# One decoder step on one core: staging of the cache keys, the layer norm's place, and the order of the prompt's score maps

## The chip, the core and the metric

The kernel runs on one core of a Trainium2 chip. The metric is the device time of one execution in microseconds (us), median of three runs. Engines are named as the profile names them: PE (TensorE) with its weight load PEld, DVE (VectorE), ACT (ScalarE), POOL (GpSimd) and SP (SyncE), which issues most transfers. Each engine works through its own program in order; semaphores order them against each other.

## The reference

One inference step of a one-layer hybrid decoder, in float32, for a prompt of 1024 tokens and for 8 samples of 8 new tokens with 1024 cached positions each:

```
xn = RMSNorm(x);  z = xn @ w_in      # 2560 columns: q 512, k 512, v 512, u 512, va 512
B: for each of 4 heads, two maps m = 1, 2 of 64 dimensions:
     p_m = softmax(q_m k_m^T / 8 + rel)          # causal; rel is a bias by distance
     o   = (p_1 - lambda * p_2) v;  RMSNorm(o) per head * (1 - lambda_init)
A: u, va = GELU(..);  u * (tril(W_s[g]) LayerNorm(va) + b[g])   # chunks of 128 positions, 4 groups
x = x + RMSNorm(concat(B, A) @ w_out)
x = x + RMSNorm((silu(g) * u') @ w_down), (g, u') = conv3(RMSNorm(x) @ w_up)
```

The samples attend to `cache_k[page_table]` and `cache_v[page_table]`: 64 pages of 128 tokens x 512 columns (256 KB a page), and to their own keys. k, v, the convolution's state and the samples' normalised va rows are outputs too.

## The kernel before

Products are made of three matmuls each: an operand is split into a rounded part and the rest (`_hi`, `_lo`), and hi x hi, hi x lo and lo x hi are added in PSUM. Tokens: 1088 columns, the samples' 64 first; nine tiles (`STEPS`), eight of 128 prompt rows and one of the samples' 64.

**Projections.** The 2560 columns of w_in are ten groups of 256: va 0, va 1, u 0, u 1, k 0, k 1, q 0, q 1, v 0, v 1 (`GROUPS`). A va or v group is nine jobs (one for each token tile, 24 matmuls of 256 columns), the other groups six jobs (24 matmuls of about 364 columns). Between the k jobs stand the nine gate jobs (the spatial product of A, one for each tile), between the q jobs the nine krow jobs (k turned for its output). Each job has a PSUM bank, the eight in turn; ACT takes the banks of va, u and krow (L941, L947, L952), DVE those of k, q, v and gate. At the first job of a group, ACT and DVE split the weights of the next one (L741, L747), whose raw halves SP loads two places ahead.

Beside this the samples' cached keys are brought into the layout that their scores need. 32 pairs of pages go through: SP loads a pair (`load_pair`, L784 on, into `k_tok[0]` or `k_tok[2]`, from pair 25 on into `k_tok[0]` alone), DVE transposes it in blocks of 32 into `k_tok[1]` (`turn_pair`, L1534 on), ACT stores it to `keys_t` in HBM (`store_pair`). `PAIR_SETS` and `PAIR_AT` say at which job: five pairs in each of the groups va 1 to k 1, four in q 0, three in q 1. In all three programs the pair stands at its job's place: DVE's transpose waits for all stores before it, ACT's store for the transpose, and ACT has it before the take of the next job.

The layer norm of va stands on DVE at the first job of u 0: for each tile `layer_stats` (DVE), a root (POOL), `center` (DVE), gain and bias (POOL, L1372 and L1374), one tile after the other. The gate jobs need its result.

**Attention.** 32 steps (`NSTEP`): four heads of eight query tiles; a step's width is 1 to 8 key tiles (ascending, in the last head descending). Steps over four tiles are wide and have a far part (banks 0 and 2) and a near part (1 and 3) for each map. For a step: PE makes the scores of both maps (`scores`); DVE takes the far part's minimum (`far_max`, L1553), adds the bias to the near part and takes its minimum (`near_max`, L1562); ACT takes exponents with row sums (`exponent`, L1027); DVE mixes the maps (`mix`, L1572 to L1577); PE turns the mix (`turn`), ACT copies it (`take_turned`, L1037), PE multiplies it with v (`weigh`, L2210); ACT squares the output (`out_square`, L1043), POOL makes the factor (L1391 to L1395), DVE scales it (`out_norm`, L1584). The scores of a step wait until both exponents of the last user of their bank are done. PE's order in step i: scores(i), the samples' scores of half a unit (`smp_scores`, L2247), weigh(i-2), turn(i-1). weigh(i-2) waits for out_norm(i-3). ACT: out_square(i-3), take_turned(i-2), exponent(i, 0), exponent(i, 1). DVE: where the scores have a free bank early, near_max(i, 0) or both far_max; mix(i-1); then the minima that are left, with out_norm(i-3) among them.

The samples' keys come back from `keys_t` in 16 units of 1 MB (`load_keys`, L810 on): unit 0 into `kt_first`, the others in turn into `kt_a`, `kt_mid`, `kt_b`, which lie in the place of the low parts of the activations and so are free only when all jobs are done. Unit u is used in steps 2u and 2u+1 (unit 0 in step 1). The cached values come in eight loads of 2 MB (`load_values`), two places.

Behind it stand w_out (L2338), the FFN (L2395, L2460) and the last norms, which the change leaves as they are.

## Time and profile before

| | us |
|---|---|
| median of 3 runs (1407.11 to 1408.3) | 1407.67 |
| the profiled execution | 1407.97 |
| its span | 1406.2 |
| PE busy in the span | 1331.6 (95%) |
| DVE, ACT, POOL busy | 722.5, 445.1, 168.7 |
| mean granted clock of TensorE | 0.981 |

Projections: the last v job begins at 318.98 us; attention: to 489.27 us, where the first product with w_out stands in the chain; w_out: to 603.29 us; then the FFN. The span is what the profile shows of one execution, from its first to its last instruction; the device time is 1.77 us longer. Busy is a union of times; PE and PEld overlap. In the tables of windows the counts in brackets are instructions, the clock is the mean that was granted to TensorE (1.00 is full), and the DMA share is that of the 16 DMA engines, which can read a little over 1. In groups by line the idle time is that of the engine just before these instructions, with what ended it. A wait is put down to the last of the things waited for.

### The profile page before, as it was taken

The page shows a single profiled execution, that of the slowest core. Times are in us where ns is not written, and L with a number is a line of the kernel's source. Part 1 is how long each engine was busy: PE and PEld are TensorE (multiplying, and loading weights), DVE is VectorE, ACT ScalarE, POOL GpSimd, SP SyncE. Part 2 cuts the span into 40 slices and gives each one's busy share as a digit, 9 for nine tenths or more (in the row PEclk, how much of TensorE's full clock was granted, in tenths as well). Part 3 has the DMA queues.
Part 4 walks back from the last instruction along what each step waited for, and adds up shares of the span by engine and source line. Part 5 has one row for each costly group of instructions (what it writes and reads, how often), then busy time and mean ns, then how long its engine had stood idle before and what let it go on. Part 6 is the DMA issues. An engine that isn't in the chain of part 4 may idle for free.

```text
span 1406.2 us, 21878 instructions
## 1 busy us (share of the span) xinstructions
PE 1331.6 (95%) x8386; PEld 1199.4 (85%) x8386; DVE 722.5 (51%) x1175; ACT 445.1 (32%) x751; POOL 168.7 (12%) x323
## 2 busy tenths in 40 slices
PE   7995798997887999999999999999999999999998
PEld 6995798994564788899898989898989999999986
DVE  6432453315668756455645454545453635454456
ACT  6301101203555754335131323232323223232332
POOL 2253000002222221120000000000000000000003
PEclk9998799998999999999999999999999999999999
DMA  7525676638879453242111110202020201110116
GB/s 261 167 75 172 226 226 206 197 88 222 212 178 269 126 171 120 83 120 75 31 60 30 40 50 21 69 15 75 15 75 15 74 15 60 30 60 27 48 46 131
DMA packets 115672, 146.97 MB, mean 105 GB/s; under 512 B 8012, under 2 KB 83445, under 8 KB 115605
## 3 DMA queue, kind: packets, MB, share of 16 engines
q1 hardware_dynamic: 107865, 122.30, 29.5%
q10 hardware_dynamic: 6748, 20.24, 4.0%
q0 software_dynamic: 992, 3.54, 1.5%
q8 instruction: 42, 0.69, 0.2%
q14 instruction: 25, 0.20, 0.0%
HBM read 114.06 MB, written 31.47 MB: 103 GB/s over the span
## 4 chain that ended last, share of the span: by engine, by line
PE 77%; DMA 7%; DVE 6%; POOL 4%; issue 3%; ACT 1%; SPq 1%; ACTq 0%; DVEq 0%; POOLq 0%
PE PS L2395 37%; PE PS L2460 16%; PE PS L2117 8%; PE PS L2338 7%; DMA keys_t<-k_tok 6%; DVE k_tok L1542 2%; PE PS L2210 2%; PE PS L2475 2%; PE PS L2490 2%; POOL small L1393 1%; DMA x_in<-in_x_prompt_dram 1%; PE PS L2270 1%; PE PS L2172 1%; POOL va L1372 1%; DVE w_lo L747 1%
## 5 line engine op out<-in xcount | busy, mean ns | idle before, releaser
L2395 PE MATMUL PS<-act_lo,wu_hi 128*128 128x364 f32 (+1 forms) x1056 | 346.4, 328 | 0.0
L2395 PE MATMUL PS<-act_hi,wu_lo 128*128 128x364 f32 (+1 forms) x1056 | 346.0, 328 | 0.0
L2395 PE MATMUL PS<-act_hi,wu_hi 128*128 128x364 f32 (+1 forms) x1056 | 345.9, 328 | 0.0
L2395 PEld LDWEIGHTS PS<-act_hi,wu_hi 128*128 128x128 f32 x1056 | 198.5, 188 | 0.5
L2395 PEld LDWEIGHTS PS<-act_lo,wu_hi 128*128 128x128 f32 x1056 | 198.1, 188 | 0.4
L2395 PEld LDWEIGHTS PS<-act_hi,wu_lo 128*128 128x128 f32 x1056 | 198.3, 188 | 0.0
L1877 DVE TENSOR_TENSOR y_acc<-y_acc,PS 128x512 f32<-128x512 f32 x162 | 111.2, 686 | 116.0 <-PE PS L2460 116.0
L2460 PE MATMUL PS<-wd_hi,g_hi 128*128 128x512 f32 x324 | 130.1, 402 | 0.0
L2460 PE MATMUL PS<-wd_lo,g_hi 128*128 128x512 f32 x324 | 128.0, 395 | 0.0
L2117 PE MATMUL PS<-act_hi,w_hi 128*128 128x364 f32 (+1 forms) x288 | 99.6, 346 | 20.7 <-DVE w_lo L747 10.0
L2460 PE MATMUL PS<-wd_hi,g_lo 128*128 128x512 f32 x288 | 114.0, 396 | 0.0
L1263 ACT CAST g_hi<-conv 128x1088 fp32r<-128x1088 f32 x21 | 23.1, 1102 | 245.8 <-PE PS L2460 189.7
L2117 PE MATMUL PS<-act_lo,w_hi 128*128 128x364 f32 (+1 forms) x288 | 97.5, 339 | 0.0
L2117 PE MATMUL PS<-act_hi,w_lo 128*128 128x364 f32 (+1 forms) x288 | 97.4, 338 | 0.0
L1435 POOL COPY stT<-hsw 128x32 f32 (+1 forms) x22 | 12.6, 571 | 696.8 <-DVE conv L1913 654.7
L1902 DVE SCALAR_TENSOR_TENSOR conv<-h_gate,cwi,conv 128x1023 f32<-128x1023 f32 x22 | 28.3, 1285 | 131.8 <-ACT conv L1251 131.8
L1542 DVE STREAM_TRANSPOSE k_tok<-k_tok 128x1024 f32<-128x1024 f32 x32 | 39.8, 1244 | 101.4 <-DMA keys_t<-k_tok 68.8
L2117 PE MATMUL PS<-w_hi,act_hi 128*128 128x256 f32 x288 | 82.0, 285 | 2.2 <-DVE act_lo L1492 1.3
L2117 PE MATMUL PS<-w_hi,act_lo 128*128 128x256 f32 x288 | 80.9, 281 | 0.0
L2117 PE MATMUL PS<-w_lo,act_hi 128*128 128x256 f32 x288 | 80.4, 279 | 0.0
L2460 PEld LDWEIGHTS PS<-wd_hi,g_hi 128*128 128x128 f32 x324 | 60.8, 188 | 21.5 <-DVE y_acc L1877 8.3
L1027 ACT ACTIVATE prob<-PS,small 128x128 f32<-128x128 f32 (+7 forms) x64 | 47.3, 740 | 91.9 <-DVE small L1562 46.0
(287 smaller groups left out, 2319.9 us busy)
## 6 DMA issues: line engine op xcount, KB each, us to landing
wu_raw<-in_w_up_dram SPq DMA_DIRECT2D x44, 512.0 KB, 3.8
k_tok<-in_cache_k_dram SPq DMA_DIRECT2D x64, 256.0 KB, 3.2
keys_t<-k_tok ACTq DMA_DIRECT2D x32, 512.0 KB, 2.9
vpage<-in_cache_v_dram SPq DMA_DIRECT2D x64, 256.0 KB, 3.9
wd_raw<-in_w_down_dram SPq DMA_DIRECT2D x22, 512.0 KB, 5.3
w_raw<-in_w_in_dram SPq DMA_DIRECT2D x20, 512.0 KB, 6.3
kt_a<-keys_t SPq DMA_DIRECT2D x20, 256.0 KB, 5.4
kt_mid<-keys_t SPq DMA_DIRECT2D x20, 256.0 KB, 7.2
```

What stands on the lines that cost most here:

```text
L1027: nc.scalar.activation(dst, score_cols(i, m), ACT.Exp, scale=-1.0, bias=nmax[:, i % 4, m:m + 1], accum_out=prob_sum[:, i % 4, m:m + 1]).th ...
L1263: nc.scalar.copy(g2_hi[e][:, NS:] if last else g_hi[:, e, NS:], conv[:, 1, :]).then_inc(g_hi_ready, 1)
L1542: nc.vector.transpose(turned, blocks).then_inc(ktok_turned, 1)
L1877: nc.vector.tensor_tensor(dst, dst, PS[:, 6 + half, :], ALU.add).then_inc(ybank_free, 1)
L1902: nc.vector.scalar_tensor_tensor(conv[:, half, NS + 1:], h[:, NS:NTOK - 1], w1, conv[:, half, NS + 1:], ALU.mult, ALU.add).then_inc(tap1_r ...
L2117: mm = nc.tensor.matmul(out, lhs, rhs, start=(i == 0), stop=(i == len(pairs) - 1))
L2210: mm = nc.tensor.matmul(PS[:, out_bank(i), 0:DV], at_sb[:, i % 2, P * k:P * k + P], v_all[:, k, DV * h:DV * h + DV], start=(k == 0), stop= ...
L2338: mm = nc.tensor.matmul(PS[:, Y_BANK[t % 2] + half, :], a[:, k, wide(TILES[t])], w[:, 512 * half:512 * half + 512], start=(first and j == ...
L2395: mm = nc.tensor.matmul(PS[:, 3 * half + c, 0:kept(c)], a[:, half, k, :], b[:, k, KEPT[c]], start=(j == 0), stop=(j == len(parts) - 1))
L2460: mm = nc.tensor.matmul(PS[:, 6 + half, :], g, w[:, e, 512 * half:512 * half + 512], start=(j == 0), stop=(j == len(parts) - 1))
L2475: nc.tensor.matmul(PS[:, LAST_BANK[t % 4] + half, :], g, w[:, e, 512 * half:512 * half + 512], start=(j == 0), stop=False)
L2490: mm = nc.tensor.matmul(PS[:, LAST_BANK[t % 4] + half, :], g, w[:, 512 * half:512 * half + 512], start=False, stop=(e == 1 and j == len(pa ...
```

## The change

- Three places for loaded pairs instead of two: `k_tok[0..2]` where q will lie (pairs 0 to 24), `k_tok[3..5]` where va lay (pairs 25 to 31). The load of pair 25 waits for all gates and for the store of the samples' va. Pair n is loaded when pair n-3 is transposed.
- Two places for transposed pairs (`k_turned`); the transpose waits for the store two before. ACT issues a store one job later.
- Tile s of the layer norm stands at the job 1 + s behind the first of u 0, its centering one job later.
- Unit 1 of the keys has its own place (`kt_second`, in the place of `vpage1`) and is loaded when group v 1 begins; the others follow in turn in `kt_mid`, `kt_b`, `kt_a`. The load of values 1 waits for the samples' scores of step 3.
- `scores` goes map by map; each map waits only for its own map's exponent of the bank's last user.
- DVE takes the first map's minimum (and out_norm(i-3)) before the mix of the last step.
- ACT squares output i-2 between the two exponents of step i.
- PE makes the samples' scores before the prompt's in each step from 2 on that isn't a multiple of 4.

```diff
-    k_tok = [at("k_tok0", 2 * ACT_BYTES + 1024, [P, 2, 512]), at("k_tok1", SCRATCH, [P, 2, 512]),
-             at("k_tok2", keep.at, [P, 2, 512])]
+    k_turned = [at("k_turned0", 2 * ACT_BYTES + 1024, [P, 2 * 512]), at("k_turned1", SCRATCH, [P, 2 * 512])]
...
+    k_tok = [at(f"k_tok{i}", a + 4096 * (i % 3), [P, 2, 512]) for i, a in enumerate(3 * [R0] + 3 * [R2 - STEPS * AW * 4])]
...
-    kt = [kt_first] + [kt_a, kt_mid, kt_b] * 5
+    kt = [kt_first, at("kt_second", V1, [P, 2, 4, 2, H, 32])] + [kt_mid, kt_b, kt_a] * 5
...
-    TOK_OF = [2 * (n % 2) if n < 25 else 0 for n in range(NPAIR)]
+    NQ_PAIR = 25
+    TOK_OF = [n % 3 if n < NQ_PAIR else 3 + n % 3 for n in range(NPAIR)]
...
+    NORM_AT = [first_of[2] + 1 + s for s in range(STEPS + 1)]
...
         def load_pair(n):
             b = TOK_OF[n]
-            if tok_uses(n):
-                sp.wait_ge(ktok_turned, max(m for m in range(n) if TOK_OF[m] == b) + 1)
-            else:
+            if n == 0:
                 sp.wait_ge(nrm_ready, STEPS)
+            if n == NQ_PAIR:
+                sp.wait_ge(gate_mul, STEPS)
+                sp.wait_ge(sgu_stored, 16)
+            if n >= 3:
+                sp.wait_ge(ktok_turned, n - 2)
...
         def load_keys(u):
-            if u == 1:
-                sp.wait_ge(kt_loaded[0], 64)
-            if u >= 4:
+            if u in (2, 3):
+                sp.wait_ge(kt_loaded[u - 2], 64)
+            if u >= 5:
                 sp.wait_ge(sscore_ready, 2 * (u - 3) + 2)
...
             elif b == 0:
                 sp.wait_ge(gated_kept, AG)
+            else:
+                sp.wait_ge(sscore_ready, 4)
...
         load_keys(0)
+        sp.wait_ge(job_ready, first_of[len(GROUPS) - 1])
+        load_keys(1)
...
         sp.wait_ge(job_ready, len(jobs))
-        load_keys(1)
...
-            if n in PAIR_AT:
-                store_pair(PAIR_AT.index(n))
+            if n - 1 in PAIR_AT:
+                store_pair(PAIR_AT.index(n - 1))
...
         for i in range(NSTEP):
-            if i >= 3:
-                out_square(i - 3)
...
             if i >= 1:
                 exponent(i, 0)
+                if 2 <= i < NSTEP - 1:
+                    out_square(i - 2)
...
         def turn_pair(n):
             b = TOK_OF[n]
-            dve.wait_ge(slot_loaded[b], 48 + 32 * (tok_uses(n) + 1))
-            if n >= 1:
-                dve.wait_ge(ktok_stored, 16 * n)
+            dve.wait_ge(slot_loaded[b % 3], slot_count(n))
+            if n >= 2:
+                dve.wait_ge(ktok_stored[n % 2], 16 * (n // 2))
...
-                if g == 2:
-                    for s in range(STEPS):
-                        layer_stats(s)
-                        if s >= 1:
-                            center(s - 1)
-                    center(STEPS - 1)
...
             if n in PAIR_AT:
                 turn_pair(PAIR_AT.index(n))
+            if n in NORM_AT:
+                s = NORM_AT.index(n)
+                if s < STEPS:
+                    layer_stats(s)
+                if s >= 1:
+                    center(s - 1)
...
         for i in range(NSTEP):
-            if i >= 2 and early(i):
+            if i >= 2:
                 if wide_step(i):
                     far_max(i, 0)
-                    far_max(i, 1)
+                    if early(i):
+                        far_max(i, 1)
+                    if i >= 3:
+                        out_norm(i - 3)
+                    near_max(i, 0)
                 else:
-                    near_max(i, 0)
-            if i == 3:
-                out_norm(i - 3)
+                    if i - 1 not in JOINED:
+                        near_max(i, 0)
+                    if i >= 3:
+                        out_norm(i - 3)
             if i >= 1:
                 mix(i - 1)
...
+            if i >= 2:
                 if wide_step(i) and not early(i):
-                    far_max(i, m)
...
+                    far_max(i, 1)
+                if i - 1 in JOINED:
+                    near_max(i, 0)
+                near_max(i, 1)
...
-            for j, (c, e) in enumerate(parts):
...
-                user = bank_user(i, 1 if second_bank(i) else j)
-                if user >= 0:
-                    pe.wait_ge(prob_ready, 2 * user + 2)
-                for m in range(2):
-                    d = slice(DH * m, DH * m + DH)
+            for m in range(2):
+                d = slice(DH * m, DH * m + DH)
+                for j, (c, e) in enumerate(parts):
...
+                    user = bank_user(i, 1 if second_bank(i) else j)
+                    if user >= 0:
+                        pe.wait_ge(prob_ready, 2 * user + m + 1)
...
+        def samples_first(i):
+            return i >= 2 and i % 4 != 0
+
         for i in range(NSTEP):
+            if samples_first(i):
+                smp_scores(i)
             if i in PARTED:
                 scores(i, 1)
...
-            if i >= 1:
+            if i >= 1 and not samples_first(i):
                 smp_scores(i)
```

## Rows read from the trace of the kernel before

**Rows 1.** Windows from:to, length, busy PE PEld DVE ACT POOL, clock, DMA share, GB/s

```profile
46.40:110.70 64.30, 64.30 (x457) 64.04 (x456) 21.70 (x34) 9.21 (x19) 24.40 (x32) 1.00 0.38 124
110.70:230.00 119.30, 89.27 (x507) 87.76 (x507) 53.37 (x63) 14.03 (x21) 8.04 (x9) 0.86 0.67 218
...
320.00:340.00 20.00, 13.29 (x144) 7.00 (x143) 10.63 (x39) 8.06 (x33) 5.84 (x9) 0.74 0.88 189
340.00:489.20 149.20, 126.45 (x1311) 84.51 (x1311) 104.61 (x294) 88.73 (x240) 38.71 (x82) 0.99 0.77 202
...
130.00:140.00 10.00, 2.04 (x13) 1.74 (x11) 1.64 (x3) 2.29 (x4) 0.00 (x0) 0.78 0.81 277
...
340.00:360.00 20.00, 15.57 (x118) 9.63 (x118) 15.26 (x39) 11.78 (x29) 5.33 (x11) 1.00 1.08 299
...
490.00:500.00 10.00, 9.93 (x51) 7.92 (x51) 8.44 (x24) 7.50 (x21) 3.04 (x6) 1.00 0.94 320
```

**Rows 2.** Waits of PE by length: total, times, longest

```profile
PE PS L2172 <- ACT prob L1027: 10.9, 13, 1.0
PE PS L2117 <- DVE w_lo L747: 10.7, 2, 10.0
PE PS L2210 <- DVE o_nrm L1584: 9.3, 16, 1.0
PE PS L2117 <- ACT uT L947: 7.4, 1, 7.4
PE PS L2095 <- DVE kT L1718: 6.2, 1, 6.2
...
PE PS L2247 <- DMA kt_a<-keys_t: 4.5, 1, 4.5
...
PE PS L2247 <- ACT s_prob L1065: 2.5, 3, 1.0
```

**Rows 3.** Groups by line in the projections: count, busy, mean ns, idle before, releasers

```profile
L1542 DVE STREAM_TRANSPOSE k_tok<-k_tok 128x1024 f32<-128x1024 f32 x32 | 39.8, 1244 | 101.4 <-DMA keys_t<-k_tok 68.8 <-DMA k_tok<-in_cache_k_dram 32.5
...
L947 ACT ACTIVATE uT<-PS 128x364 f32<-128x364 f32 (+1 forms) x12 | 5.7, 473 | 79.7 <-DVE k_tok L1542 79.3 <-PE PS L2117 0.4
```

**Rows 4.** Chain that ended last: start, length, engine or transfer

```profile
54.41 2.93 DMA keys_t<-k_tok
...
67.33 7.17 DMA keys_t<-k_tok
...
82.35 1.29 POOL va L1372
...
111.91 1.27 POOL va L1372
...
221.43 5.38 PE PS L2117 x24
227.24 3.94 PE PS L2117 x24
...
339.54 0.56 POOL small L1393
```

**Rows 5.** DMA issues: size and median time to landing

```profile
keys_t<-k_tok ACTq DMA_DIRECT2D x32, 512.0 KB, 2.9
```

**Rows 6.** Busy time of each engine in three steps of the second head

```profile
386.26:391.41 5.15, 3.80 (x29) 2.31 (x29) 3.77 (x10) 2.80 (x8) 1.45 (x3) 1.00 1.09 296
391.41:397.08 5.67, 4.35 (x32) 2.65 (x32) 4.18 (x11) 3.19 (x9) 1.58 (x3) 1.00 1.00 280
397.08:403.20 6.12, 5.44 (x39) 3.40 (x39) 5.61 (x13) 4.04 (x10) 1.72 (x3) 1.00 0.67 152
```

**Rows 7.** Groups by line, in the attention

```profile
L1027 ACT ACTIVATE prob<-PS,small 128x128 f32<-128x128 f32 (+7 forms) x64 | 47.3, 740 | 91.9 <-DVE small L1562 46.0 <-PE PS L2117 43.6 <-DVE prob L1577 2.2
...
L1393 POOL TENSOR_TENSOR small<-small 128x1 f32<-128x1 f32 x32 | 27.8, 869 | 2.7
L1577 DVE SCALAR_TENSOR_TENSOR prob<-prob,small,prob 128x128 f32<-128x128 f32 (+7 forms) x32 | 27.0, 843 | 1.1
```

More of the change, by code:

```diff
@@ L517, in _program @@
     ktok_turned = sem("ktok_turned")
-    ktok_stored = sem("ktok_stored")
+    ktok_stored = [sem(f"ktok_stored{i}") for i in range(2)]
     kt_loaded = [sem(f"kt_loaded{i}") for i in range(3)]
@@ L631, in _program, with slot_count, kt_count @@
     PAIR_AT = [jobs_of(k + 1)[j * len(jobs_of(k + 1)) // len(pairs)] for k, pairs in enumerate(PAIR_SETS) for j in range(len(pairs))]
-    def tok_uses(n):
-        return TOK_OF[:n].count(TOK_OF[n])
+    NORM_AT = [first_of[2] + 1 + s for s in range(STEPS + 1)]
+    def slot_count(n):
+        return 48 + 32 * (sum(b % 3 == TOK_OF[n] % 3 for b in TOK_OF[:n]) + 1)
     def kt_place(u):
-        return max(u - 1, 0) % 3
+        return (u - 2) % 3 if u >= 2 else u
+    def kt_count(u):
+        return 64 * (sum(kt_place(v) == kt_place(u) for v in range(u)) + 1)
     ring, ring_taken = [], []
@@ L834, in _ @@
         sp.wait_ge(w_lo_ready, 2 * len(GROUPS))
-        sp.wait_ge(ktok_stored, 16 * NPAIR)
+        for i in range(2):
+            sp.wait_ge(ktok_stored[i], 16 * NPAIR // 2)
         load_keys(0)
+        sp.wait_ge(job_ready, first_of[len(GROUPS) - 1])
+        load_keys(1)
         v_jobs = [n for n, job in enumerate(jobs) if job[0] == "v"]
```

22 lines of the change are left out of this document (8 added, 14 removed).

## The prediction

> **What bounds the kernel now.** I read the page first: PE is busy 95% of the span, so what can be won is PE's idle time and the time in which it runs below full clock. The table of windows says where that is: between 110.7 and 230.0 us PE is busy 89.27 of 119.30 us at a mean granted clock of 0.86, between 320 and 340 us 13.29 of 20 at 0.74, and from 340 to 489.2 us, the rest of the attention, 126.45 of 149.20 at 0.99; from 46.4 to 110.7 it has no idle time at all [rows 1]. The change does not touch what comes behind the attention. Then the waits by length name what ends each idle stretch [rows 2].
>
> In the projections these waits (w_lo 10.7, uT 7.4, kT 6.2 us) are not the work of those operations. VectorE's 32 transposes L1542 take 39.8 us and have 101.4 us of idle before them, 68.8 of it until the last store `keys_t<-k_tok` has landed, and ScalarE's 12 evictions L947 wait 79.3 us for such a transpose [rows 3]. All transposes write one tile, so each waits for the store before it; ScalarE, which issues the store, waits for the transpose before it may take PE's next bank. The chain in order of time shows the store's 2.93 to 7.17 us, and between them nine tiles of layer norm: 82.35 to 111.91 is seven of them, 4.22 us each [rows 4]. No pair of pages moves in that time. PE runs 8 banks ahead, then stands.
>
> In the attention the waits are 10.9 us for `prob` (a step's scores wait until the exponents of both maps of the step before have freed the banks), 9.3 us for `o_nrm` (a head's output waits for ScalarE's square, POOL's root and VectorE's scale), 4.5 us once for `kt_a`, 2.5 us for `s_prob` [rows 2].
>
> **The change, part by part.**
>
> *Projections: staging and layer norm.* Removed are the wait of a transpose for the store just before it (now for the one two before) and of a load for one of two places (now three). A store is issued one job later, so ScalarE takes PE's bank first. No instruction is added. PE then waits only if the mean pace of pairs is below its own. Its u job is 24 matmuls at 3.94 us [rows 4]. The ring that is left: the next job must end (4.0) and be taken (about 0.5), store n-2 lands after 2.9 by median [rows 5], transpose n takes 1.24 [rows 3]: 8.6 us for two pairs, against two jobs at 4.0 and a sixth job in each group without a pair. It fits; a store of 7.17 is 4 us late once, and the 8 banks cover it. The layer norm keeps POOL's lockstep of 4.22 us a tile, from about 83 to 125 us, now beside the pairs; its last tile is due for a gate in k1, after 150. Were that cover gone, a gate would wait a tile, 4 us. On SP's queue pair 25 is held until all gates are done and `sgu` is stored; behind it stand the weight halves of the last groups, due some 25 us later: nothing.
>
> So the idle time 119.30 - 89.27 = 30.0 us should go [rows 1], and the low clock with it. In the chain the first projection after the stall before 220 us takes 5.38 us, the next, of the same 24 matmuls, 3.94 [rows 4]; a mean of 0.86 lies between the levels 1.2 and 2.4 GHz, and the low one came behind idle stretches. The clock's cost is at most 89.27 x 0.14 = 12.5 us, and at least 5 restarts x 1.44 = 7.2; I take 9. For what stays (the first key rows wait for the last k eviction, perhaps a gate) I leave 1. Sum: 30 + 9 - 1 = 38 us, bounds 25 (the pairs keep the pace in part) and 41.
>
> *Keys of the second unit* get a place of their own and are loaded during v1. The wait of 4.5 us goes, and some of the low clock behind it: in 320 to 340 that costs at most 13.29 x 0.26 = 3.5 us [rows 1, 2]. I take 4.5 + 1 = 5.5; bounds 3 (the start's own chain of exponent, mix and turn is late next) and 8. Values 1 now wait on SP's queue until unit 1 is used (step 3), with the keys of unit 5 behind them; both are due at steps 9 and 10: nothing.
>
> *Scores map by map, the first map's minimum before the mix, the square a step earlier, the samples' scores first.* The idle time from 340 us on is 149.20 - 126.45 = 22.75 us [rows 1]. Three steps of the second head, cut at their mixes of 640, 768 and 896 columns: spans 5.15, 5.67, 6.12 us; PE busy 3.80, 4.35, 5.44; VectorE 3.77, 4.18, 5.61; ScalarE 2.80, 3.19, 4.04 [rows 6]. After the change a step cannot be shorter than VectorE's work and its handovers, some 0.4 us: 4.2, 4.6, 6.0, or about 0.95, 1.05 and 0.1 less than now; the fourth wide step is like the third, with a gap for `s_prob`.
>  Does a ring forbid it? Map 1: its exponents end, then mix (0.84 mean, 0.4 with its two small ones), half of VectorE's other work (1.4), an exponent (0.74 + 0.2) [rows 6, 7]: with handovers 4.1 us in the middle step: below 4.6. The new one: ScalarE's square stands between the exponents of the two maps and waits for the weighing, which stands behind map 1's scores on PE. That is at most 2.7 of PE's 4.35 to 5.44, a square and an exponent (0.5 and 1.0): 4.2, while PE has a turn, the samples' scores and map 0's scores of the next step to do. It fits too.
>  The `o_nrm` wait (9.3) goes whole, since POOL's 0.87 mean [rows 7] and its two short ones now have a step's time. Of the `prob` wait (10.9) the samples' and map 0's scores fill about half; of `s_prob` (2.5) I count nothing. 9.3 + 5 = 14 us of the 22.75. Bounds: 3 (the waits only change places) and 20.
>  POOL's root L1393 takes 0.56 us at 339.54 but 0.87 in the mean, in steps where VectorE mixes [rows 4, 7]. The Trainium skill (SBUF — State Buffer, on the shared port pair) says that a GpSimd operation and a VectorE operation with two SBUF inputs exclude each other for a whole instruction; the mix is such a one, and the trace agrees. By that rule a root can still be held by a mix after the change; that would be some 0.5 us inside the slack of a step, and where one were late again it would be a part of rival B.
>
> *Sum.* 38 + 5.5 + 14 = 57.5 us. The profiled execution took 1407.97 us, 1.77 over its span; the median of the runs is 1407.67, 0.3 less. 1407.97 - 57.5 - 0.3 = 1350. What is behind only moves forward. The last values and rows of w_out, whose transfers fill 490 to 500 us (320 GB/s, share 0.94 [rows 1]), hang on the last steps' products, and that tail gets hardly shorter.
>
> **Rivals.**
> *A, the pairs keep part of the pace.* A pair moves 1.05 MB; with the weights that is 18.9 MB in va1, u0 and u1. PE does these in 64.3 us less one va job (2.8) and plus three u jobs (12) [rows 1]: 73.5 us, 257 GB/s. The stretch with pairs shows 218 GB/s in the mean and 277 at a share of 0.81 at best [rows 1]. At 218 they would be 13 us late, and the stalls of u1 and k0 come back: 12 us less gain, 1362. The Trainium skill (DMA: Bandwidth & Descriptors, Issuing engines are not separate DMA queues) has it that DMAs of all issuing engines interleave on the same 16 engines: more places give no rate once the share is full, as in 340 to 360 us with 299 GB/s at 1.08 [rows 1]; the trace agrees, but the stretches with pairs are below that. Chance 0.14.
> *B, the attention gains only its key wait.* Map 1's exponents then wait for the weighing, or VectorE's order sets the step: 14 becomes 1: 1363. For it: VectorE is within 0.2 us of PE in all three steps [rows 6]. Against: it idles up to 1.5 us a step. Chance 0.14.
> *C, slower.* The ring of staging: a store held a job longer, transpose and load behind it. PE has 181 us for 32 pairs, 5.65 each (projections to the end of q1). Each pair over that costs PE 32 times the excess; 58 us are eaten at 1.8 us, when the ring takes 2 x 7.45 = 14.9 us, which needs stores of 9.2 us instead of 2.9. At 10 us it is 1350 + 32 x 2.2 = 1420. The longest store in the chain has 7.17 [rows 4]. Chance 0.03. That the change does nothing, because something else holds PE at the same places: 1407, 0.01.
> *D, all idle time goes:* 41 + 8 + 20: 1339. Chance 0.13.
>
> **The numbers.** Forecast 0.55 (its own range 1342 to 1358), A 0.14, B 0.14, D 0.13, C 0.03, nothing 0.01. Range 1337 to 1368. A measurement of this kernel tells 0.2% (3 us) from no change: faster 0.96, within it 0.01, slower 0.03.
>
> **What would show it.** PE without idle and at clock 1.00 from 46 us to the end of the projections, at about 283 instead of 322 us; L1542 idle for loads or for nothing; L947 waiting for PE alone; layer norm between transposes, to about 125 us. No wait of L2247 for keys, none of L2210 for `o_nrm`, half of L2172's 10.9 us; wide steps of 4.2, 4.6, 6.0 us; PE's first L2338 near 431. Wrong in the first part if uT or w_lo still end waits of several us; in the third if PE's idle time from the fourth step on stays above 15 us.

## The result

| | before | after |
|---|---|---|
| median of the runs | 1407.99 us (1407.11 to 1408.31) | 1370.55 us (1369.76 to 1374.39) |
| profiled execution, its span | 1407.97, 1406.2 | 1369.76, 1368.0 |
| start of the samples' own scores (end of the projections) | 321.95 | 282.39 |
| from there to the first product with w_out | 167.3 | 169.0 |
| from there to the end of the span | 916.9 | 916.6 |

The ratio is 0.974 (95% interval 0.9721 to 0.976): faster, by 37 us instead of the forecast 57.5, and outside the range. The three parts of the table say where. The projections gained 39.6 us (forecast 38), the rest behind the attention moved forward unchanged, and the attention, which was to lose 19.5 us (5.5 for the keys, 14 for the new orders), became 1.7 us longer. One of the four executions of e12 below took 2351 us, in a slow state of the chip, and is not counted.

Windows of the changed kernel, with the columns of [rows 1]: the projections as there, ten of their microseconds, and the whole attention.

```profile
46.40:110.70 64.30, 64.30 (x460) 64.25 (x458) 28.40 (x35) 14.69 (x28) 16.86 (x21) 1.00 0.71 236
110.70:230.00 119.30, 119.30 (x755) 118.76 (x754) 60.67 (x80) 15.18 (x21) 20.48 (x21) 1.00 0.73 246
...
190.00:200.00 10.00, 10.00 (x64) 9.95 (x64) 2.22 (x3) 1.17 (x2) 0.00 (x0) 1.00 0.96 348
282.39:451.38 168.99, 150.31 (x1436) 98.33 (x1436) 111.90 (x326) 97.02 (x274) 32.18 (x91) 0.99 0.76 196
```

And the attention of the kernel before, in the same cut:

```profile
321.95:489.27 167.32, 137.79 (x1436) 89.71 (x1436) 113.97 (x323) 96.80 (x272) 44.62 (x90) 0.96 0.80 202
```

The second row is what [rows 1] had at 89.27 us busy and a clock of 0.86: now PE has no idle time and full clock. The last row of the first fence and the row after it are the point of this case. The same 1436 matmuls keep PE busy for 150.31 us instead of 137.79, at a clock no lower. Its idle time did fall, from 29.5 to 18.7 us, and 12.5 us of busy time came in its place. A look at idle time alone would have called this a success.

The groups that answer to [rows 3, 5, 7] (line, operation, count, busy, mean ns, idle before and its end; the last row is DMA issues):

```profile
L1557 DVE STREAM_TRANSPOSE k_turned<-k_tok 128x1024 f32<-128x1024 f32 x32 | 39.3, 1234 | 21.8 <-DMA keys_t<-k_turned 21.8
L1408 POOL TENSOR_TENSOR small<-small 128x1 f32<-128x1 f32 x32 | 18.4, 576 | 2.7
L961 ACT ACTIVATE uT<-PS 128x364 f32<-128x364 f32 (+1 forms) x12 | 5.7, 474 | 38.1 <-PE PS L2134 38.1
keys_t<-k_turned ACTq DMA_DIRECT2D x32, 512.0 KB, 4.1
```

The transposes wait 21.8 us instead of 101.4, ScalarE's takes wait for PE alone. The waits of PE by length, to be set against [rows 2]:

```profile
PE PS L2287 <- ACT s_own L1095: 4.2, 3, 1.5
PE PS L2215 <- DVE prob L1592: 4.0, 8, 1.5
PE PS L2227 <- DVE o_nrm L1599: 3.9, 7, 1.1
PE PS L2189 <- ACT prob L1042: 3.6, 3, 1.5
```

Above them stands 5.4 us for `rel_rep` at the very start, as before (5.2). `prob` fell from 10.9 to 3.6, `o_nrm` from 9.3 to 3.9, the keys' 4.5 is gone; new is `s_own`, three times about 1.4. The three steps of [rows 6], cut at the same mixes:

```profile
345.69:350.91 5.22, 4.78 (x28) 2.50 (x27) 3.82 (x10) 2.97 (x9) 0.93 (x3) 1.00 1.06 314
350.91:356.51 5.60, 5.60 (x33) 3.12 (x32) 4.22 (x10) 3.13 (x8) 0.93 (x3) 1.00 1.03 257
356.51:362.25 5.74, 4.15 (x36) 3.41 (x39) 4.53 (x13) 5.03 (x13) 0.93 (x3) 1.00 1.00 205
```

Forecast were 4.2, 4.6 and 6.0 us. In the middle one PE is busy for all of its 5.60 us, where [rows 6] have 4.35. Where the busy time comes from stands in the timeline of the scores of a 1024-column step (start, length, operation, count), first of the kernel before, then of the changed one, with the end of map 1's exponent on ScalarE:

```profile
397.10 1.99 PE L2172 MATMUL PS<-kT,qT 64*128 64x512 f32 x8 [1.00 <-ACT prob L1027]
```

```profile
353.36 3.17 PE L2189 MATMUL PS<-kT,qT 64*128 64x512 f32 x8
...
354.30 0.19 ACT L1042 ACTIVATION_READ_ACCUMULATOR prob<-PS,small 128x1 f32 x1
```

Eight equal matmul records (two for each matmul of the program) take 1.99 us in the one and 3.17 in the other. Map 0 of a head contracts over rows 0 to 63 of the array and map 1 over rows 64 to 127. Before, their records start in pairs, 7 ns apart (397.099 and 397.106), and run together. After the change map 0's start at 353.358, 353.891, 354.321 and 354.750; map 1's wait for map 1's exponent, start at 354.544 and end at 356.52, so that the two overlap in part only. The Trainium skill (TensorEngine Tiling (Array Packing), Key Properties) says that tiles of the array operate independently and can execute matmuls in parallel; the trace agrees, and the prediction had not weighed it.

More busy time is not yet a longer step, though. Map 1's exponent ends at 397.04 before and at 354.49 in the changed kernel; the last score ends 2.05 us and 2.04 us behind it. In none of the 13 wide steps whose scores are issued as a whole do the two kernels differ in this by over 0.1 us. Map 0's scores only start earlier, in time in which PE would have waited for map 1's exponent. What sets the 5.60 us is a ring (a chain of waits that closes on itself, here from one mix to the next):

```profile
350.91 1.02 DVE L1592 SCALAR_TENSOR_TENSOR prob<-prob,small,prob 128x768 f32<-128x768 f32 x1
...
351.99 0.87 PE L2215 MATMUL PS<-ident,prob 128*128 128x128 f32 x6
...
352.79 0.64 PE L2264 MATMUL PS<-kt_a,qp 128*32 128x256 f32 x8
...
355.38 0.75 DVE L1577 CUSTOM_DVE_ANT_0 PS<-PS,bias_sb,far_min 128x512 f32<-128x512 f32 x1
...
356.51 1.15 DVE L1592 SCALAR_TENSOR_TENSOR prob<-prob,small,prob 128x896 f32<-128x896 f32 x1
```

The mix of a step, its turn on PE, the samples' scores and map 0's scores of 353.36 behind it in PE's program, map 0's minimum as soon as they end (355.38), and the next mix, which now stands behind that minimum. In the kernel before, the chain that ended last has neither PE nor a mix in this stretch (start, length):

```profile
391.38 0.36 ACT PS L1043 x2
...
392.09 1.22 POOL small L1393
...
393.87 0.62 DVE PS L1562
...
394.54 0.56 DVE far_min L1553
...
396.85 0.19 ACT prob L1027
```

From the end of map 1's exponent to the end of the next one, 391.38 to 397.05, it goes over the square, POOL's factor, `out_norm`, the minima of both maps and map 1's exponent: 5.67 us, the length of the middle step in [rows 6].

### The profile page after: what moved, and what is told of

It reads as the page before. It is cut to its first block, busy times and chain, and to the rows that moved or that the text cites. A ratio compares the mean times of both kernels' runs of the same rounds, so it can differ in the third digit from the quotient of the medians.

```text
span 1368.0 us, 21879 instructions
## 1 busy us (share of the span) xinstructions
PE 1334.0 (98%) x8386; PEld 1199.9 (88%) x8386; DVE 720.4 (53%) x1175; ACT 445.5 (33%) x751; POOL 159.8 (12%) x323
## 4 chain that ended last, share of the span: by engine, by line
PE 92%; DVE 3%; issue 2%; ACT 1%; DMA 1%; SPq 0%; POOL 0%; POOLq 0%; DVEq 0%; ACTq 0%
PE PS L2418 38%; PE PS L2134 17%; PE PS L2483 16%; PE PS L2361 7%; PE PS L2189 3%; PE PS L2227 2%; PE PS L2498 2%; PE PS L2513 2%; PE PS L2264 1%; PE PS L2215 1%; PE PS L2287 1%; DVE prob L1592 1%; PE PS L2119 1%; DMA x_in<-in_x_prompt_dram 1%; PE PS L2352 1%
## 5 line engine op out<-in xcount | busy, mean ns | idle before, releaser
L2134 PE MATMUL PS<-act_hi,w_hi 128*128 128x364 f32 (+1 forms) x288 | 95.8, 333 | 0.0
L2134 PE MATMUL PS<-act_lo,w_hi 128*128 128x364 f32 (+1 forms) x288 | 94.4, 328 | 0.0
L2134 PE MATMUL PS<-act_hi,w_lo 128*128 128x364 f32 (+1 forms) x288 | 94.4, 328 | 0.0
L2483 PEld LDWEIGHTS PS<-wd_lo,g_hi 128*128 128x128 f32 x324 | 60.9, 188 | 12.3
```

The costliest lines, as they stand in the source:

```text
L2134: mm = nc.tensor.matmul(out, lhs, rhs, start=(i == 0), stop=(i == len(pairs) - 1))
L2483: mm = nc.tensor.matmul(PS[:, 6 + half, :], g, w[:, e, 512 * half:512 * half + 512], start=(j == 0), stop=(j == len(parts) - 1))
```

## The experiments

Attention is the time from the own scores to the first w_out product; idle is PE's in it; scores is the union of the 192 prompt score matmuls. Clock is the mean granted to TensorE in the attention. The last two columns are the third and the last head (steps 17 to 24 and 25 to 32, each from the end of one weighing to the end of the next, the first one counted from the own scores). All from the profiled execution, the time is the median. "Base" in the list means the changed kernel's projections and keys with the attention of before.

| kernel | time | attention | idle | scores | clock | third head | last head |
|---|---|---|---|---|---|---|---|
| before | 1408.0 | 167.3 | 29.5 | 40.6 | 0.96 | 44.5 | 40.6 |
| changed | 1370.6 | 169.0 | 18.7 | 54.4 | 0.99 | 44.5 | 47.0 |
| e1 changed, pairs with one wait | 1386.0 | 184.5 | 41.4 | 42.0 | 0.96 | 49.8 | 50.3 |
| e2 before, map by map | 1407.1 | 168.3 | 29.9 | 40.3 | 0.96 | 44.6 | 40.8 |
| e3 base | 1363.7 | 163.6 | 26.5 | 39.6 | 0.98 | 44.6 | 40.6 |
| e4 changed, pairs with own waits | 1372.9 | 173.6 | 20.2 | 54.5 | 0.97 | 45.4 | 46.2 |
| e5 base + map by map, own waits | 1362.7 | 163.8 | 16.4 | 51.3 | 0.98 | 44.6 | 40.6 |
| e6 base + early square | 1367.8 | 166.2 | 31.7 | 39.6 | 1.00 | 45.5 | 45.6 |
| e7 base + minimum ahead of mix | 1387.3 | 186.3 | 39.2 | 44.3 | 0.94 | 49.7 | 50.2 |
| e8 base + samples first | 1365.8 | 165.4 | 29.4 | 39.6 | 0.99 | 45.1 | 41.4 |
| e9 changed, mix first | 1368.4 | 167.7 | 25.3 | 48.3 | 1.00 | 45.7 | 45.4 |
| e10 base + early square in part | 1361.8 | 163.3 | 24.7 | 40.6 | 0.97 | 44.2 | 40.6 |
| e11 e10 + map by map, own waits | 1359.8 | 159.0 | 13.1 | 52.5 | 1.00 | 44.2 | 40.6 |
| e12 changed, layer norm in a block | 1383.1 | 169.0 | 18.7 | 54.4 | 0.99 | 44.5 | 47.0 |
| e13 e11 + minimum ahead of mix | 1366.3 | 166.1 | 9.1 | 58.8 | 0.97 | 42.5 | 50.5 |
| e14 e11, second unit's keys late | 1365.4 | 165.2 | 17.5 | 53.4 | 0.98 | 44.2 | 40.6 |
| e15 before + layer norm spread | 1376.9 | 166.6 | 30.5 | 40.6 | 0.97 | 44.5 | 40.6 |

The clock is a cause of its own in this list. The 15th step of the kernel before takes 1.2 us more than its 7th, which has the same products, and the clock is low in it (columns as in [rows 1]):

```profile
358.74:364.96 6.22, 4.13 (x40) 3.06 (x38) 5.23 (x22) 4.18 (x13) 1.85 (x3) 1.00 1.03 206
401.78:409.22 7.44, 5.66 (x39) 4.24 (x38) 6.39 (x27) 4.19 (x13) 1.85 (x3) 0.77 0.63 136
```

e15, with the same attention, has 6.22 us in both, e3 7.48 in both at a clock of 0.77. Which execution has it where is not explained by any edit here. Behind the first two steps the clock is full throughout in e6, e9 and e11, and in all third heads but those of e1 (23rd step 0.81) and e7 (24th, 0.81), so the third heads are the cleanest comparison: there the four edits together cost nothing (44.5 against 44.6 us), and what the changed kernel loses to e3 stands in the last head.

**e1: the changed kernel with the scores in pairs.** The loop of before inside the changed kernel: part by part, both maps together, after the exponents of both.

```
-            for m in range(2):
-                ...
-                for j, (c, e) in enumerate(parts):
-                    ...
-                        pe.wait_ge(prob_ready, 2 * user + m + 1)
+            for j, (c, e) in enumerate(parts):
+                ...
+                    pe.wait_ge(prob_ready, 2 * user + 2)
+                for m in range(2):
```

> The changed kernel with the order of the score products as before: for each part both maps one behind the other, and the wait for both exponents of the bank's last user. All else as changed. Theory 1 (the two maps read rows 0 to 63 and 64 to 127, and their matmuls ran at the same time as long as they stood next to each other; map by map they run one after the other in wide steps): the union of the score matmuls in the attention falls from 53.4 us to about 40, and the time from 1370.5 to 1357 to 1361. Theory 2 (the score order costs nothing; the square between the exponents and the minimum before the mix set the steps): 1368 to 1372.

Measured 1386.0 us, ratio 0.9854 (0.9814 to 0.9893): above both expectations. The pairs are back (scores 42.0) and the attention is 15.5 us longer. So the lost pairs can't be the cause alone: something else in the changed attention is very dear once the scores wait for both maps (e7 finds it). Its waits: `prob` 19.5 us, `prob` ahead of the turn 7.1.

**e2: the kernel before with the scores map by map**, under the wait of before.

```
-            for j, (c, e) in enumerate(parts):
+            for m in range(2):
+                ...
+                for j, (c, e) in enumerate(parts):
                     ...
                     pe.wait_ge(prob_ready, 2 * user + 2)
-                for m in range(2):
```

> The kernel before with one edit: scores map by map, still with the wait for both exponents. Theory 1: 20 wide steps of two parts lose the overlap, 0.45 to 0.9 us each on a path that has little slack: union from 39.7 to about 53 us, time 1408 to between 1416 and 1422. Theory 2: within 2 us of before, as no instruction and no wait is added.

1407.1 us, ratio 0.9995 (0.9979 to 1.001). The order of issue does nothing. The timeline row:

```profile
398.29 1.99 PE L2172 MATMUL PS<-kT,qT 64*128 64x512 f32 x8 [1.00 <-ACT prob L1027]
```

It is still 1.99 us, against the first expectation: the records start in pairs 13 ns apart (398.291, 398.305), although in the program all of map 0's matmuls stand ahead of map 1's. What takes the pair apart is thus the wait between the maps.

**e3: the changed projections and keys, all four attention edits undone.**

> The changed kernel with all attention edits but the keys' own place taken back (score order, minimum, square, samples' scores as before). Both theories: the projections' 39.6 us stay, and the keys' wait of 4.5 us and its low clock go: 1408 - 39.6 - 5.5 = 1363, so below the changed kernel. Theory 1 puts it above run e1 (the other orders gain a few us: 1363 against 1359), theory 2 puts it 7 us below e1.

1363.7 us (1360.98 to 1365.67), ratio 0.9682 (0.9646 to 0.9718): some 7 us below the changed kernel. Projections and keys do what was forecast (1407.97 - 38 - 5.5 = 1364.5), and the four attention edits together cost 7 us by the medians. In the profiled executions the attention differs by 5.4 us (169.0 against 163.6), and e3's own scores started 1.7 us earlier with the same projections.

**e4: pairs, but each map with its own wait** (the loop of e1 with `2 * user + m + 1`).

> As run e1, but each map waits only for its own exponent; the parts are still the outer loop. Theory 1: where map 1's exponent is late, map 0's far part starts alone and that pair is lost, the near pair is kept: union 40 to 47 us, time 1357 to 1364. Theory 2: as e1.

1372.9 us, ratio 0.9745 (0.9711 to 0.9778); scores 54.5. Above the first expectation. Same as the changed kernel in its pairing, as e2 leads one to expect: with a wait of its own map 1 comes later whatever the order. Its 7th, 8th and 15th steps, at a clock of 0.71 to 0.86, are together 4.7 us longer than the changed kernel's.

The next four put one attention edit each on the base of e3.

**e5: map by map with own waits.** The first loop of the diff of e1, turned round.

> The kernel with the changed projections and the attention of before (1363.7 us), with one attention edit put back: the scores go map by map, each map waiting for its own exponent. Theory A (lost pairs): the wait between the maps takes them apart, so the union of the score matmuls rises from 39.6 us to over 50 us, the idle time of TensorE falls by about as much, and the time stays within 1362 to 1369. Theory B (the square ahead of map 1's exponent is what costs): the edit alone gains what the prediction gave it, some 4 us: 1358 to 1361. Theory C (TensorE's own wait was never the bound): union and idle unchanged, 1363 to 1365.

1362.7 us (1361.34 to 1364.45), ratio 0.968 (0.9662 to 0.9699). Waits of PE in e3, then in e5:

```profile
PE PS L2187 <- ACT prob L1042: 11.3, 14, 1.0
PE PS L2225 <- DVE o_nrm L1599: 10.3, 16, 1.2
```

```profile
PE PS L2225 <- DVE o_nrm L1599: 10.9, 18, 1.2
...
PE PS L2187 <- ACT prob L1042: 0.6, 2, 0.3
```

The wait for `prob` falls by 10.7 us, the score matmuls take 11.7 us more, the time is the same. The numbers are the first expectation's; its reason, that the lost pairs eat up a gain, is not what the trace shows. The scores that moved now run during the wait, and the last score still ends 2.03 us behind map 1's exponent. Neither kernel's chain goes over this wait: between two wide steps both have the ring of the kernel before, from exponent over square, POOL's root and the minima to exponent, without PE (in e5 from 346.78 to 352.45, 5.67 us as before). An eleven-microsecond wait was filled, and it had cost nothing.

**e6: the early square.**

```
-            if i >= 3:
-                out_square(i - 3)          # head of step i
                 exponent(i, 0)
+                if 2 <= i < NSTEP - 1:
+                    out_square(i - 2)
                 exponent(i, 1)
```

> The same base (1363.7 us) with the square of step i-2 between the two exponents of step i as the only attention edit. Theory B: ScalarE waits there for the weighing, map 1's exponent and with it the next pair of scores come later, and every wide step grows: 1374 to 1386, with over 15 us of idle time ahead of the squares. Theory A: ScalarE has slack, 1362 to 1366. Theory D (the edit gains, since the square no longer stands at the head of the step): 1356 to 1361.

1367.8 us, ratio 0.9725 (0.9707 to 0.9743): 4 us slower than e3. Steps are counted here from the end of one weighing to the end of the next, 1 to 32: the 7th shrinks from 7.48 to 5.78 us, and the 9th and 17th grow from 6.33 to 7.87, the 28th from 7.66 to 8.97. The time lies above the expectation of slack in ScalarE and below that of a cost in every wide step. The last head is 5.0 us longer in all. Of the 7th's gain 1.26 us is the clock, which was 0.77 in e3. In the 9th, 17th and 28th ScalarE also copies the samples' probabilities. The changed kernel has the same; its timeline there:

```profile
368.10 2.05 PE L2227 MATMUL PS<-v_all,at_sb 128*128 128x128 f32 x16
...
370.19 0.34 ACT L1058 ACTIVATE PS<-PS,small 128x128 f32<-128x128 f32 x1 [1.86 <-PE PS L2227]
...
370.55 0.46 ACT L1042 ACTIVATE prob<-PS,small 128x256 f32<-128x256 f32 x1
...
371.46 0.21 ACT L1095 COPY s_own<-PS 64x64 f32<-64x64 f32 x1
...
371.72 1.93 PE L2287 MATMUL PS<-vpage,s_at 128*8 128x128 f32 x64 [1.46 <-ACT s_own L1095]
```

The square waits for the weighing, and behind it in ScalarE's program stand map 1's exponent and the two sample copies (`s_at`, `s_own`), for which PE then waits. In e3 `s_own` is copied at 367.58, while PE weighs.

**e7: the minimum ahead of the mix.** VectorE's loop of the changed kernel on the base of e3 (in its core):

```
             if i >= 2:
+                    near_max(i, 0)         # needs scores(i)
             if i >= 1:
                 mix(i - 1)
-                near_max(i, 0)
                 near_max(i, 1)
```

> The same base (1363.7 us) with VectorE's order of the changed kernel (first map's minimum ahead of the last step's mix) as the only attention edit. Theory A and the prediction: map 0's exponent starts earlier, but TensorE waits for both exponents, so 1361 to 1365. Theory E (the mix comes later and the turn on TensorE waits for it, the time's new bound): the wait for prob ahead of the turn rises from under 1 us to over 5 us in sum and the time to 1368 to 1376. Theory B expects 1361 to 1366.

1387.3 us (1386.79 to 1388.38), ratio 0.9859 (0.9843 to 0.9876): 23.6 us slower than e3, more than any expectation. Its chain of waits over one wide step (start, length):

```profile
351.10 0.88 DVE prob L1592
351.99 0.61 DVE far_min L1568
...
352.73 0.49 DVE PS L1577
...
354.12 0.20 ACT prob L1042
...
354.36 2.81 PE PS L2189 x8
...
357.91 0.23 DVE small L1589
...
358.16 1.02 DVE prob L1592
```

This is a ring of 7.06 us from mix to mix (5.15 in [rows 6] between the mixes of the same widths): the mix, map 1's minimum behind it in VectorE's program, map 1's exponent, the next scores which wait for it, map 0's minimum of these scores, and only then the next mix. Before, the mix ran beside the scores and was not in the ring. One microsecond of the 7.06 is the clock: it was 0.78 in this step, and the eight score records took 2.81 us instead of the 1.77 of the same step in e3. The next step, from 358.16 to 364.94 at a clock of 0.98, takes 6.78 us against 5.67. VectorE's waits show it; in e7 from 300 us on:

```profile
DVE far_min L1568 <- PE PS L2189: 26.5, 12, 3.3
```

In e3 the same wait is 1.0 us, in the changed kernel 16.2. Of the 22.8 us by which e7's attention is longer than e3's, 12.7 are idle time and 10.1 busy time of PE, with the same matmuls at a mean clock of 0.94 instead of 0.98; e6, with its scores in pairs too and full clock, needs 134.5 us where e7 needs 147.1. So the ring and a low clock share the loss. In the seven steps of the third head that e7 has at full clock (17th to 23rd) the order alone costs 2.6 us (40.5 against 37.9). The ring also explains e1, which has this order with the wait for both maps: 1386.0.

**e8: the samples' scores first.**

```
+            if samples_first(i):           # i >= 2 and i % 4 != 0
+                smp_scores(i)
             scores(i)
```

> The same base (1363.7 us) with the sample scores ahead of the step's own scores on TensorE as the only attention edit. Theory A: TensorE fills its wait for the exponents with the sample scores, which are 1.0 to 1.4 us a step where a step has them; the step's own scores and so the exponents start no later, and the time falls to 1357 to 1361. Theory F (the sample scores wait for the keys or for the sample probabilities and hold the step's scores behind them): 1366 to 1374. Theory B: 1362 to 1365.

1365.8 us, ratio 0.9703 (0.9687 to 0.9719): 2.1 us slower if anything. `prob` falls from 11.3 to 5.9 us and `o_nrm` rises from 10.3 to 16.8: the wait moved. The time lies between the third expectation and the second.

**e9: the changed kernel with the mix first** (the diff of e7 backwards).

> The changed kernel (1370.6 us) with VectorE's order of before: the last step's mix ahead of the first map's minimum; scores map by map, early square and sample scores first stay. Theory E (the minimum ahead of the mix costs whatever else is changed, since the mix then waits for the scores of the next step; it cost 23.6 us alone): 1363 to 1368. Theory G (with a wait per map it costs nothing, the early square and the samples are what is lost: singly -1.0, +4.1 and +2.1 us on 1363.7): 1368 to 1372.

1368.4 us (1367.67 to 1369.02), ratio 0.9713 (0.9695 to 0.973). What costs 23.6 us on e3 costs 2.1 us here: map 0's scores no longer wait for map 1's exponent, so their minimum is less late (VectorE waits 16.2 us for it in all instead of 26.5), and the clock is low less often. The measured value lies just inside the second expectation and 0.4 us above the first; theory E's "whatever else is changed" is wrong. In the first three heads the order costs nothing (132.2 us with it, 133.2 without); in the last, where the changed kernel's clock was low in two steps, it costs 1.6 us.

**e10: the early square in some steps only.**

```
+        def square_early(i):
+            return 2 <= i < 24 and i not in SMP_STEP     # SMP_STEP = [9, 17, 28]
```

> Projections of the changed kernel, attention of before, and the early square only in steps before 24 that take no sample output (not in 9, 17 and from 24 on). With the early square everywhere the three steps after a turned head lost 1.7 us each less, steps 9 and 17 cost 1.54 each more and the steps from 25 on 5.5 us more. Theory H (these are separate effects): 163.6 us of attention falls by 5 to 6 us and the time to 1357 to 1360. Theory I (what is won in one step is waited for in the next): 1362 to 1365.

1361.8 us (1359.14 to 1365.71), ratio 0.9667 (0.9639 to 0.9694). Between both expectations and not told apart from e3. The steps 9, 17 and from 25 on are back at e3's lengths, but the 7th and 15th keep 7.24 and 7.08 us, at clocks of 0.78 and 0.80.

**e11: the same, map by map with own waits.**

> As the run before, with the scores map by map as well. Theory J (ScalarE and VectorE set the step; TensorE's pairing only turns idle time into busy time, as where it was alone, 1362.7 against 1363.7 us): within 2 us of the run before. Theory K (with the early square, map 0's scores come earlier and pay): 3 us or more below the run before.

1359.8 us (1358.9 to 1363.73), ratio 0.9662 (0.9639 to 0.9685): the best kernel here by its median, with an attention of 159.0 us, 4.6 less than e3; it is below the changed kernel by 10.7 us, which is clear, and below e3 by 3.9, where the runs overlap. The whole attention and the second of the three steps:

```profile
281.46:440.43 158.97, 145.90 (x1436) 95.27 (x1436) 112.78 (x323) 96.02 (x272) 36.34 (x90) 1.00 0.79 207
...
345.12:350.59 5.47, 5.35 (x34) 3.21 (x32) 4.08 (x10) 3.12 (x9) 0.93 (x3) 1.00 0.95 254
```

Against e3 PE's idle time is 13.5 us less and its busy time 8.9 us more (145.9 against 137.0). The three steps are 4.95, 5.47 and 6.31 us, shorter than [rows 6] by 0.2 at most and the last one longer; the gain is in the 7th and 15th (5.78 against 7.48) and the 2nd (3.39 against 4.03). Of the 7th's and the 15th's, 1.26 us each is e3's low clock, so of the 4.6 us some 2.1 are left for the edits (an estimate: 4.6 less twice the 7.48 - 6.22 of the steps above). Between e10 and e11 the profiled attentions differ by 4.4 us, the medians by 2.0, and the runs overlap.

**e12: the changed kernel with the layer norm as one block.**

```
             if g + 1 > split:
                 dve_split_w(dve, split)
+                if g == 2:
+                    ...                    # nine tiles, one after the other
-            if n in NORM_AT:
-                ...                        # one tile
```

> The changed kernel (1370.6 us) with the layer norm as one block of nine tiles again; three staging places stay. Theory L (the layer norm's 38 us without a transpose are what stood in the way; PE is 8 banks ahead and then stands): the own scores start 15 to 30 us later, 1385 to 1400. Theory M (the single staging tile with its wait for each store was it): they start up to 8 us later, 1371 to 1379.

1383.1 us, ratio 0.9816 (0.9794 to 0.9838). The own scores start at 297.46, 15.1 us later, as the first expectation has it, though the time stays 2 us under its range. The window of [rows 1] and the chain behind the block:

```profile
110.70:230.00 119.30, 108.09 (x657) 107.00 (x656) 63.25 (x75) 19.49 (x28) 6.75 (x8) 0.94 0.81 283
```

```profile
116.30 0.88 SPq L800
...
120.87 0.91 SPq L741
121.83 10.55 DMA w_raw<-in_w_in_dram
...
134.76 7.04 PE PS L2134 x24
```

The pairs' loads stand in SP's queue until the block is over and VectorE transposes again; the next weights stand behind them, and their transfer then shares the rate with the pairs that follow: 10.55 us, while the core's transfers together ran at 375 GB/s and a share of 1.02. So the norm's block reached PE through the weights.

**e15: the kernel before with the layer norm spread**, the single staging tile kept.

> The kernel before (1407.7 us) with the layer norm's tiles spread over the jobs, the staging tile as before. The run with the new staging and the norm in one block showed the block to be worth 15 us of the 39.6. Theory S (two separate delays that add up): 1391 to 1395. Theory T (with one staging tile the pairs are late anyway, so the norm between them gains less and adds a late gate): 1396 to 1408.

1376.9 us (1376.05 to 1378.61), ratio 0.9791 (0.9769 to 0.9814), below both expectations. Own scores at 290.98: 31.0 us earlier than before.

```profile
110.70:230.00 119.30, 111.92 (x699) 111.14 (x698) 59.13 (x78) 14.94 (x21) 18.27 (x22) 0.97 0.68 219
```

The staging alone gives 24.5 us (321.95 - 297.46), the spread alone 31.0, both 39.6. They are not two separate delays: either lets the pairs catch up with what the other loses.

**e13: e11 with the minimum ahead of the mix.**

> The kernel of the part-wise early square and map-by-map scores (1359.8 us; own scores to w_out 159.0 us) with the first map's minimum ahead of the last step's mix as the only further edit. Theory E (the minimum waits for scores, and only a wait for both maps makes these late): with a wait per map it costs little, 1358 to 1363, with wide steps longer by 0.5 us and narrow ones shorter by 0.4 us, as in the changed kernel against its version with the mix first. Theory N (the order costs whatever the wait): 1370 or more.

1366.3 us, ratio 0.9708 (0.9685 to 0.973): 6.5 us slower than e11, between the two expectations. In the attention the edit costs 22.8 us on e3, 7.2 on e11 and 1.3 on e9. In a head the 10th to 12th steps are 1.0, 0.4 and 0.2 us shorter and the 13th is 0.5 longer, about as expected; the third head is the shortest of all, 42.5 us against 44.2. The loss is in the 7th step (7.50 against 5.78 us, clock 0.77) and in the last head (steps 26 to 29: 6.31, 9.25, 8.18, 6.59 us against 5.07, 6.00, 7.66, 3.34), where the clock was full in the 26th and 0.87, 0.94 and 0.74 in the next three. How much of that is the order and how much the clock stays open. This kernel has the least idle time of all, 9.1 us, and is 6.5 us slower than the best.

**e14: e11 with the second unit's keys loaded after the last projection.**

```
-        sp.wait_ge(job_ready, first_of[len(GROUPS) - 1])
-        load_keys(1)
         ...
         sp.wait_ge(job_ready, len(jobs))
+        load_keys(1)
```

> The same kernel of 1359.8 us with the keys of the second unit loaded where they were before, after the last projection, though they have their own place. Theory P (the prediction: the place earns 5.5 us, of which 4.5 is the wait): first step 11 us instead of 6.1, 1364 to 1366. Theory R (the value pages, which no longer compete with them, or the next waits take it back): within 1.5 us, 1358 to 1361.

1365.4 us (1365.19 to 1368.45), ratio 0.9712 (0.9688 to 0.9736): 5.6 us slower, the first step 11.67 us instead of 6.11.

```profile
PE PS L2267 <- DMA kt_second<-keys_t: 5.2, 1, 5.2
```

## Why the prediction was right and wrong

- *Projections, 38 us (bounds 25 to 41): right.* 39.6 measured, with PE at full clock and without idle in both windows. The ring of two pairs fits. The store's median rose from 2.9 to 4.1 us and the transposes still wait 21.8 us, and the eight banks cover it. What the prediction did not say is how the term divides between staging and layer norm; e12 and e15 show that 24.5 and 31.0 overlap by 15.9.
- *Keys of the second unit, 5.5 us: right.* e14 measures 5.6.
- *Rival A, the rate of the transfers:* refuted. PE has no idle time in either window of the projections, and the changed kernel moves 348 GB/s in the window from 190 to 200 us with PE fully busy, above the 257 that it asked for.
- *Attention, 14 us (bounds 3 to 20): this step failed.* With the keys' first step apart (10.99 to 6.11 us, 4.9 less), the four orders made the attention 6.6 us longer; e3 against the changed kernel says 5.4 us in the profiled executions and 7 by the medians. Four parts of it failed.
  - "Of the `prob` wait (10.9) the samples' and map 0's scores fill about half" gave 5 of the 14 us. The wait was filled, and it was worth nothing, since the ring that set the wide steps (square, POOL's factor, `out_norm`, minima, exponent: 5.67 us) does not go over PE. e5 isolates it: 11 us less waiting, 12 us more busy time, the same time.
  - "The `o_nrm` wait (9.3) goes whole" took the length of a step after it from VectorE's work alone, 4.6 us in the middle step. With the square taken early POOL's root does leave the ring, but the next ring is hardly shorter. In e11 it is 5.46 us in that step: map 1's exponent ends at 344.64, the mix, a minimum, `out_norm` and map 0's minimum take until 347.59, and both exponents with the square between them until 350.10. In the changed kernel it is the ring over the mix, 5.60 us.
  - The rings were checked for map 1 and for the square, not for the mix. Placed behind a minimum that waits for scores, the mix enters the ring. That is 23.6 us alone (e7, in part by a low clock), though only 2.1 in the changed kernel, where map 0's scores don't wait for map 1's exponent (e9).
  - "It fits too", of the square between the exponents, was worked out for a wide step. It does not hold where ScalarE has the samples' outputs to copy: `s_own` 4.2 us, the 9th and the 17th step 1.5 us longer each in e6 and not in e10. The last head is 5.0 us longer in e6.
- *What of the 14 us was to be had?* e11, without the costs of the last two kinds: 4.6 us of attention against e3, some 2.1 of them if e3's low clock is taken out. Its idle time falls by 13.5 us, close to the 14 that were counted, and 8.9 come back as busy time, mostly map 0's scores in what was a wait. The idle time was sized well and was not the thing to size.
- *The clock in the attention* was reckoned for its first steps only. In e3 it is low in two later steps, in e7 in six, and in the changed kernel in two of the last head (29th and 30th: 0.93 and 0.80). What part of the changed kernel's 6.4 us in the last head against e3 is the clock's is not shown.
- *Bounds.* The prediction took "the waits only change places" (+3) as the low end. Nothing excluded a loss; with one of 7 us in place of 3 the sum would have been 38 + 5.5 - 7 and the forecast's high end 1371, which holds the result.
- *Rival B* (1363: "map 1's exponents then wait for the weighing, or VectorE's order sets the step") is the nearest of all. Squares wait 20.5 us for weighings in the changed kernel, against 10.8 before. It put the cost at the gain's size, not beyond it.
- *The signs named in advance.* PE's idle time from the fourth step on should be below 15 us; it is 150.90 - 136.57 = 14.3 (window 300.5 to 451.4), so this sign passed although the step failed. The first w_out product came at 451.38 instead of 431, and the step lengths missed: those were the signs that told.
- *POOL's root.* Its mean fell from 869 to 576 ns. In e3 the chain shows it beside a mix of 1.02 us, and the changed kernel's timeline has it clear of the mix:

```profile
346.98 1.21 POOL small L1408
```

```profile
352.89 0.55 POOL L1408 TENSOR_TENSOR small<-small 128x1 f32<-128x1 f32 x1
```

  The rule of the Trainium skill that the prediction cited (SBUF — State Buffer, on the shared port pair) is borne out by both. Taking the square early moved the root out of the mix's time; `o_nrm` still ends 7.6 us of waits in e11.

## What to carry to other kernels

Before splitting or filling a wait, see whether it stands in the ring that sets the step: a wait outside it is worth nothing, however long it is in sum. Where the matmuls behind it use different halves of the array, splitting it turns idle time into busy time and does not move the end of the last one, so judge by the length of a step and not by idle or busy time. When an instruction is moved on an in-order engine, write down the ring through it anew for every kind of step, with what it now stands behind; an order that costs 2 us with one wait costs 24 with another. Put an edit on and off alone before believing a sum of edits, and compare steps at the same granted clock: one low-clock step here is 1.3 us.

## What the runs showed of the hardware

- Matmuls on rows 0 to 63 and on rows 64 to 127 ran together though the program had all of one half ahead of all of the other (e2: starts 13 ns apart, eight records in 1.99 us), as long as no wait stood between them. With a wait of its own the second half began 1.19 us later and the eight took 3.17 us; in both cases the last ended some 2.04 us behind the exponent that the second half waited for.
- The same step of one kernel took 6.22 us at full clock and 7.44 at a mean clock of 0.77 (before, 7th and 15th step), with PE busy 4.13 and 5.66 us.
- The core's transfers reached 348 GB/s at a share of 0.96, while PE worked at full clock without a gap; the fastest stretch shown of before had 320 at 0.94 [rows 1]. With PE less busy e12 had 375 at 1.02 for 10.6 us.
- A 512 KB store took 4.1 us by median in this traffic instead of 2.9 [rows 5], and a weight transfer behind held-up pairs 10.55 us (e12).
